# A hybrid encoder layer on one core: order of the first loads, weights and half products

## What is computed

```python
h = rmsnorm(x, norm_mix_w)              # rows scaled by rsqrt(mean square), columns by a weight
proj = h @ w_in                         # split into GLA q, k, v, gate, ga (16 wide), and attention parts
g = log_sigmoid(ga @ w_alpha2 + b_alpha2) / 16
o_gla = gla_chunked(gq, gk, gv, g)      # linear attention with the decay exp(cumsum(g))
o_diff = diff_attention(rope(dq), rope(dk), dv, lam)
x = x + concat(o_gla, o_diff) @ w_out   # after head norms and SiLU gates
x = x + cross_attention(rmsnorm(x), rmsnorm(mem)) @ w_co
return rmsnorm(x, final_norm_w)
```

## Time and profile before

| | value |
|---|---|
| median of 3 runs | 829.70 us |
| profiled execution, its own time | 829.52 us |
| its span, first to last instruction | 827.7 us |
| TensorE busy | 814.0 us, 98% of the span |
| VectorE busy | 585.9 us, 71% |
| ScalarE busy | 436.0 us, 53% |
| GpSimd busy | 84.2 us, 10% |
| chain that ended last | TensorE 92%, VectorE 4%, ScalarE 1%, DMA 1% |

### The profile page before, as it was taken

The page is one execution under the profiler, slowest core; times in us unless marked ns, Lnnn a source line. Parts: engine busy times, 40 slices in busy tenths (PEclk is TensorE's granted clock), DMA queues, the critical chain, the costliest instruction groups (busy, mean ns, idle before and its releaser), DMA issues.

```text
span 827.7 us, 13216 instructions
## 1 busy us (share of the span) xinstructions
PE 814.0 (98%) x4586; PEld 683.9 (83%) x4586; DVE 585.9 (71%) x1360; ACT 436.0 (53%) x1057; POOL 84.2 (10%) x123
## 2 busy tenths in 40 slices
PE   8999999999999999999999999999999999999996
PEld 7887888888788888888888898888888888888885
DVE  6788677776578678767857877599835564367997
ACT  7865445444345445445545676544645454366443
POOL 3100121211001011111100000010010000001201
PEclk9999999999999999999999999999999999999999
DMA  8321369972133245645512268955332121206945
GB/s 298 105 83 39 97 184 195 187 134 66 52 118 109 87 76 106 131 91 110 107 61 84 62 207 255 278 146 127 129 101 71 45 65 41 87 13 137 216 94 203
DMA packets 70409, 99.21 MB, mean 120 GB/s; under 512 B 6596, under 2 KB 38472, under 8 KB 70344
## 3 DMA queue, kind: packets, MB, share of 16 engines
q1 hardware_dynamic: 52360, 64.29, 24.3%
q0 software_dynamic: 15392, 29.36, 19.7%
q10 hardware_dynamic: 2592, 4.72, 1.7%
HBM read 83.68 MB, written 31.46 MB: 139 GB/s over the span
## 4 chain that ended last, share of the span: by engine, by line
PE 92%; DVE 4%; ACT 1%; issue 1%; DMA 1%; SPq 0%; ACTq 0%
PE bank L1841 14%; PE bank L1843 14%; PE bank L1842 14%; PE banks2to L1841 10%; PE banks2to L1843 10%; PE banks2to L1842 10%; PE banks6to L1913 4%; PE banks2to L2100 3%; PE bank L2123 2%; DVE neg_max L1640 2%; PE banks2to L2036 1%; PE bank L2125 1%; PE banks6to L2060 1%; DVE w_lo L1379 1%; PE banks6to L1843 1%; PE banks6to L1841 1%
## 5 line engine op out<-in xcount | busy, mean ns | idle before, releaser
L1843 PE MATMUL bank<-w_hi,actT_lo 128*128 128x512 f32 x412 | 161.2, 391 | 0.0
L1841 PE MATMUL bank<-w_hi,actT_hi 128*128 128x512 f32 x384 | 154.8, 403 | 0.2
L1842 PE MATMUL bank<-w_lo,actT_hi 128*128 128x512 f32 x384 | 149.6, 390 | 0.0
L1379 DVE SCALAR_TENSOR_TENSOR w_lo<-w_raw,vecs,w_hi 128x512 fp32r<-128x512 f32 x120 | 86.8, 749 | 28.1 <-ACT w_hi L1097 28.1
L1843 PEld LDWEIGHTS bank<-w_hi,actT_lo 128*128 128x128 f32 x412 | 77.3, 188 | 16.9
L1097 ACT ACTIVATE w_hi<-w_raw,vecs 128x512 fp32r<-128x512 f32 x120 | 82.6, 720 | 8.4 <-DMA w_raw<-in_w_ckv 4.3
L1841 PEld LDWEIGHTS bank<-w_hi,actT_hi 128*128 128x128 f32 x384 | 73.0, 190 | 15.1 <-DVE w_lo L1379 1.5
L1842 PEld LDWEIGHTS bank<-w_lo,actT_hi 128*128 128x128 f32 x384 | 72.3, 188 | 13.4
L983 POOL TENSOR_TENSOR rs_o<-var_o,neg_half 128x1 f32<-128x1 f32 (+1 forms) x48 | 29.5, 615 | 375.2 <-DVE var_o L1667 256.9
L1843 PE MATMUL banks2to<-w_hi,actT_lo 128*128 128x512 f32 x164 | 64.0, 390 | 0.0
L1262 ACT ACTIVATE prob<-banks2to,neg_maxs 128x128 f32<-128x128 f32 (+7 forms) x64 | 47.0, 741 | 15.2 <-DVE neg_maxs L1641 15.0
(11 more groups left out here) (368 smaller groups left out, 2045.1 us busy)
## 6 DMA issues: line engine op xcount, KB each, us to landing
w_raw<-in_w_in SPq DMA_DIRECT2D x56, 256.0 KB, 3.4
out_sums<-in_w_out POOLq DMA_DIRECT2D x11, 1024.0 KB, 10.6
late_sums<-in_w_co POOLq DMA_DIRECT2D x11, 1024.0 KB, 9.3
w_raw<-in_w_ckv SPq DMA_DIRECT2D x32, 256.0 KB, 3.3
w_raw<-in_w_cq SPq DMA_DIRECT2D x32, 256.0 KB, 2.8
stage_in<-in_x SPq DMA_DIRECT2D x8, 512.0 KB, 4.4
tile_a<-mixed ACTq DMA_DIRECT2D x16, 256.0 KB, 3.4
x_res<-in_x SPq DMA_DIRECT2D x8, 512.0 KB, 6.3
```

The costliest lines, as they stand in the source:

```text
L1379: return dve.scalar_tensor_tensor(dst, src, scale, hi.bitcast(F32), ALU.mult, ALU.subtract)
L1841: pe.matmul(dst, l_hi, r_hi, start=start, stop=False)
L1842: pe.matmul(dst, l_hi, r_lo, start=False, stop=False)
L1843: return pe.matmul(dst, l_lo, r_hi, start=False, stop=stop)
```

## The change

The hand-written list and the first loads are put in another order. (a) ScalarE's queue issues the loads of the three norm weights and the GLA head norm weight; SP keeps positions, diff norm weight and bias. (b) SP loads x tiles 0 and 1, the small loads, then weight 0, x 2, weight 1, x 3, weights 2 and 3, and `ga_raw` behind them (before: x 0 to 2, small loads, weight 0, x 3, weight 1, `ga_raw`, weights 2 and 3). (c) `pos` and `vec` come at the head of the list, after 14 fillers on TensorE, ahead of the scaling of tile 0. (d) Weight 0 is split between the scalings of tiles 0 and 1. (e) Tile 2's square comes behind weight 1. (f) `G0h` 0 and 1 both stand ahead of tile 2, and there are two more, `G0h` 2 behind tile 2 and `G0h` 3 behind tile 3, with weights 2 and 3 split for them; `G0` (0,2) and `G0` (0,3), which stay where they are, so shrink to 256 tokens. 32 fillers remain of 42.

```diff
-    plan = [("zeros",), *normed(0), *normed(1), ("sq", 2), *busy(0, 24), ("tr", 0, 0), ("pos",), ("scale", 2), ("tr", 0, 1)]
-    plan += [*busy(1, 2), ("tr", 1, 0), ("vec",), ("tr", 1, 1), *busy(2, 6), ("sq", 3), ("w", 0), ("tr", 2, 0), ("scale", 3)]
-    plan += [("tr", 2, 1), *busy(3, 10), ("G0h", 0), ("w", 1), *tr(3), ("G0h", 1), ("w", 2), ("const",)]
-    plan += [*normed(4), ("w", 3), *normed(5), ("const2",), ("ga", 0)]
+    plan = [("zeros",), *busy(0, 14), ("pos",), ("sq", 0), ("vec",), *busy(1, 6), ("scale", 0), ("sq", 1), ("w", 0)]
+    plan += [("scale", 1), *tr(0), *busy(2, 4), *tr(1), *busy(3, 8), ("w", 1), ("G0h", 0), ("sq", 2), ("w", 2), ("scale", 2)]
+    plan += [("sq", 3), ("G0h", 1), *tr(2), ("scale", 3), ("w", 3), ("G0h", 2), *tr(3), ("G0h", 3), ("const",)]
+    plan += [*normed(4), *normed(5), ("const2",), ("ga", 0)]
     plan += [("G0", 0, 0), *normed(6), ("G0", 0, 1), ("z", 0), ("w", 4), *normed(7), ("gate", 0), *tr(4)]
     plan += [("w", 5), ("G0", 0, 2), *tr(5), ("w", 6), ("gsum", 0), ("G0", 0, 3), *tr(6), ("w", 7), ("G0", 0, 4), *tr(7)]
...
-            for t in range(3):
+            for t in range(2):
                 load_input(t)
             for dst, src in (
-                (vec_rows[0:8, :], a["norm_mix_w"][0].rearrange("(k p) -> k p", p=P)),
-                (vec_rows[8:16, :], a["norm_cross_w"][0].rearrange("(k p) -> k p", p=P)),
-                (vec_rows[16:24, :], a["norm_mem_w"][0].rearrange("(k p) -> k p", p=P)),
-                (vec_rows[24:25, :], a["gla_norm_w"]),
+                (pos_i[:, :], a["positions"][0].rearrange("(t p) -> t p", p=P)),
                 (vec_rows[25:26, :], a["diff_norm_w"]),
                 (vec_rows[26:28, :], a["b_alpha2"][0].rearrange("(k p) -> k p", p=P)),
-                (pos_i[:, :], a["positions"][0].rearrange("(t p) -> t p", p=P)),
             ):
                 sp.dma_start(dst, src).then_inc(d_vec, 16)
-            load_weight(0)
-            load_input(3)
-            load_weight(1)
+            for n in range(2):
+                load_weight(n)
+                load_input(2 + n)
+            for n in range(2, NRAW):
+                load_weight(n)
...
-            for n in range(2, NRAW):
-                load_weight(n)
...
+            for dst, src in (
+                (vec_rows[0:8, :], a["norm_mix_w"][0].rearrange("(k p) -> k p", p=P)),
+                (vec_rows[8:16, :], a["norm_cross_w"][0].rearrange("(k p) -> k p", p=P)),
+                (vec_rows[16:24, :], a["norm_mem_w"][0].rearrange("(k p) -> k p", p=P)),
+                (vec_rows[24:25, :], a["gla_norm_w"]),
+            ):
+                act.dma_start(dst, src).then_inc(d_vec, 16)
```

## The result

The change makes the kernel slower. The median goes from 829.68 us to 834.96 us (six executions of each, 829.51 to 830.14 and 834.07 to 835.66); the ratio is 1.0063, with a 95% interval of 1.0053 to 1.0073. The direction was forecast, the size was not: +5.3 us where +2.3 was expected, and 834.96 lies above the range, which ended at 833.9.

What follows compares the result with a forecast made beforehand. TensorE, busy 98% of the span, was taken as the bound; `ga` 2.34 us later would pass through the gate chain to tile 6 and the end, taking 829.52 to 831.9 us, range 830.2 to 833.9.

Steps and rivals of the forecast that it cites:

- The gate chain has no slack: At tile 6: `z`, gate activations and tile 4 end within 0.15 us of TensorE's list; `ga`'s +2.34 reaches the end.
- The half products gain nothing: Ahead of `ga`: 2.9 us of work done early only leaves TensorE standing 2.9 us before tile 6.
- From `G0h` 0 to `ga`: First projection: `G0h` 0 at 11.55 instead of 13.83, `ga` at 20.4 instead of 18.06, held by tile 3.
- Loads: At the beginning: the small loads let VectorE's cast run at 5.6; bounds 5.0 gives -0.15, 6.5 gives +0.85 us.
- Tiles 0 and 1 from the start of scaling 1 to both low parts: At the beginning: scaling 1 starts at 8.1 and both low parts are over 3.36 us later.
- the bounds: Late small loads -0.15 to +0.85 us; slow pace for tiles 0 and 1 0.8 to 1.3; most favourable end 828.3.
- rival (2): Gate chain sets tile 6, and TensorE also loses clock in the stall or at the beginning: 833.6 us; chance 0.15.
- No cost of the loads' order on ScalarE: At the beginning: four load issues and the table load end near 3.4, hidden before x tile 0 at 4.35.

Runs made afterwards that it cites:

- nohalf: The changed kernel without the two added half products, 12 fillers in place of each and `G0` (0,2) and (0,3) whole again; 834.20 us, ratio 1.0053.
- b_fill14: The kernel before with 14 fillers at the head instead of 24, nothing else; 830.35 us, ratio 1.0009.
- b_loads: The kernel before, its list kept, with the change's loads on both queues and in their new order; 831.26 us, ratio 1.0023.
- b_half: The kernel before with only the half products `G0h` 2 and 3 added ahead of `ga`; 835.78 us, ratio 1.0073.
- a_late: The changed kernel, reordered behind `z`: tile 4 copied before the gate's activations, two products before tile 5, weights 5 to 7 before the cumulated sum; 833.67 us, 1.0041.
- best: The changed kernel with earlier small loads, more fillers, tiles 2 and 3 earlier, no `G0h` 3, and a_late's order behind `z`; 830.86 us, ratio 1.0019.
- best2: best with all seven small loads on ScalarE's queue, fillers 20, 6, 4 and 8, tile 0 scaled ahead of the vectors' copies; 831.87 us, ratio 1.0027.
- fill: The changed kernel with 32, 10, 8 and 12 fillers instead of 14, 6, 4 and 8; 835.86 us, ratio 1.0074.
- small: The changed kernel with SP's three small loads ahead of x tile 1 instead of behind it; 834.46 us, ratio 1.0058.
- fill22: The changed kernel with 22, 7, 7 and 11 fillers instead of 14, 6, 4 and 8; 834.94 us, ratio 1.0060.
- chg_a: The changed kernel again with no edit, one more profiled execution; 835.25 us.
- chg_b: The changed kernel again with no edit, another profiled execution; 836.01 us.
- chg_c: The changed kernel again with no edit, another profiled execution; 834.65 us.
- cover: The changed kernel with the full product `G0` (0,4) moved from behind tile 6 to ahead of it; 833.40 us, ratio 1.0044.

## Why the prediction was wrong in size and right in direction

- *The gate chain has no slack, and the shift of `ga` is that of tile 6 and of the end.* Right. 2.59 us of stall were measured where 2.9 were forecast, released by the line that was named; +4.81 at `ga`, +4.83 at tile 6, +4.6 at the end. nohalf, b_fill14 and b_loads show the same equality, but with them TensorE's own list is as late as the gate chain; what tells the two apart is the stall itself, b_half, and a_late, best and best2, which break the equality.
- *The half products gain nothing.* Right, by nohalf, whose median is even 0.8 lower.
- *From `G0h` 0 to `ga`.* Right: 11.55 to 20.4 is 8.85, measured 13.85 to 22.87, 9.02. VectorE's late scaling of tile 3 (19.31) and the wait of 0.8 ahead of tile 3 (0.9 forecast) are there.
- *Loads.* The first mis-sized term. I took 5.6 for the cast, from the row of x tile 1, and it was 6.49, the upper bound of the range (6.5, +0.85). Scaling 1 began at 9.05 instead of 8.1: +0.95.
- *Tiles 0 and 1 from the start of scaling 1 to both low parts.* The second and largest: 3.36 was summed from rows at the full clock, 4.75 was measured (9.05 to 13.80), +1.39, as TensorE had half its clock from 8.21 to 11.63. The sum itself was sound: at the full clock fill, small and fill22 took 3.41 to 3.56, and the three other executions of the change 4.16 to 4.54. The row that I had, the slow pace of the first fillers, gave 0.8 to 1.3 for it, which stood among the bounds and in rival (2), not in the sum. This was the step that failed: I took the fillers that were removed (14 for 24 at the head, worth 1.0 us in the trace of b_fill14) as costing nothing, since they stood in waiting time. They were what got and kept the clock: with 20 or more at the head it had risen by 7.1 us in all nine traces and stayed up over tiles 0 and 1 in seven (not in b_loads and best2); with 14 it had risen in four of nine, and stayed up in one, small.
- *The sum.* 0.95 + 1.39 + 0.17 for the rest (of 9.02 against 8.85, less 0.04 that `G0h` 0 followed sooner) is 2.47, the difference between 20.4 and 22.87. Both terms were at about their upper bounds (0.95 against 0.85, 1.39 against 1.3); the range took these in one by one, and not the two together: 831.9 + 0.85 + 1.3 is 834.05, and the profiled execution took 834.07. They are linked: the late loads make the idle gap of 1.88 us in which the clock is lost (in chg_a it hadn't risen yet), and both small, which brings them earlier, and fill22, which fills the gap, keep it.
- *The median above the profiled execution.* Rival (2) had the price 1.7 for a clock that falls in the stall; it was 1.6 in chg_a and chg_b, and absent in two other traces of the same program. A fall in about half of the executions would put the mean 0.8 above the undisturbed ones, and the median is 0.9 above the trace without it. That this is the cause of the 0.9 is argued, not shown. Of the timed executions only the mean granted clock over the whole span is known: the three of the change at 0.995 or 0.996 took 835.09 to 835.66 us, the three at 0.997 to 0.999 took 834.07 to 834.82. This fits, but doesn't say where the clock was low, and the one at 0.999 took 834.69, so that not all of the spread is the clock's.
- *No cost of the loads' order on ScalarE.* Not seen in the change, where tile 2's square stands later in the list (13.46); with the old list the loads cost 1.6 in the median (b_loads), in its trace in part by the clock. I had left out that the two edits need each other.

## What to carry to other kernels

Look for the chain that ends together with the bound engine's own list, and ask of each moved piece of work on which side of that chain it lay: work taken from behind a wait that it covered is worth nothing ahead of it. A filler on TensorE is not free to remove because it stands in waiting time; price it by what the clock behind it costs. When two uncertain terms share a cause, here late loads and the gap that loses the clock, put both upper bounds in one case and give that a place in the range.

## What the runs showed of the hardware

- TensorE's clock fell to half behind 1.9 to 2.3 us of idling in a thinly used beginning (the change, chg_b, chg_c, best2), in b_loads within an idle time of 2.0, and stayed full with gaps of up to 0.8 and 0.4 us (small, fill22). With 14 fillers at the head and then 1.6 to 2.8 us of idling it rose for the first time only at 10.0 to 12.9 us in five traces (chg_a, cover, a_late, b_fill14, nohalf); the same program did either (the change, chg_a). In dense work a stall of 2.6 us ahead of tile 6 brought it down, in its last 0.4 us or up to 1.4 us behind it, in chg_a, chg_b, fill, small, fill22 and b_half, and left it in the change's own trace and in chg_c; a fall cost 1.3 to 1.6 us of work.
- The last of the seven small loads was in at 5.16 us with SP's three ahead of x tile 1 (small, best), at 6.49 behind it (the change; 6.2 to 7.0 in other executions with this order) and at 7.38 with all seven on ScalarE's queue (best2). The four on ScalarE's queue were issued by 2.4 in the change's trace; moving all seven there (best2) made the last one later, not earlier.
- x tile 1, used at 5.84 with the small loads behind it, was used at 6.31, 7.64 and 7.73 in three runs with them ahead of it: the price of the passing was 0.5 to 1.9 us, not a constant.
